# Hybrid decoder step on one core: scores, a square and the denominators' product between halves of turned probabilities, and the sampled part's order in the slots of a layer

## The chip, the core and the metric

The kernel runs on one core of a Trainium2 chip. The metric is the device time of one launch in microseconds (us), the median of several executions. The engines are named as in the profile: PE is TensorE (PEld its weight load), DVE VectorE, ACT ScalarE, POOL GpSimd, SP SyncE.

## The reference

One inference step of a hybrid decoder trunk of two layers, on a prompt of 1024 tokens and on 8 sampled sequences of 4 new tokens with 8192 tokens of paged cache each. What matters here is the mixer that each layer begins with:

```
p = h @ w_in                                   # one projection, columns split among three head groups
A: 8 heads, latent attention (latent 128, rotary key 32 shared by the heads)
   s  = (q_lat . ckv + q_rope . kr) * ATTN_SCALE, causal; pr = softmax(s); o = pr @ ckv
   for the samples the keys are 64 pages of 128 rows per sequence, read through page_table
B: 4 RWKV-7 heads of 64:  S <- S(diag(w) - kk^T (a*kk)) + v k^T,  y = S r, group norm, bonus, gate
C: short convolution of width 3
h = LN(alpha*h + concat(A,B,C) @ w_out);  h = LN(alpha*h + HierMoE(h))
```

All arithmetic is float32.

## The kernel before

Each of the two layers is a projection (in the first layer up to about 326 us), then the mixer, then the output projection and the routing, then 32 experts. The change touches the mixer alone, which the rows below show at 326 to 841 us and at 1768 to 2284 us.

The mixer of a layer is eight **slots** of code that is written out by hand, one function for each engine: the order in which `slot(w, x, y, t, b)` calls its steps is the order of the instructions on that engine, and the engines meet at counting semaphores (each step adds one to the semaphore of its engine and stage; tables such as `PE_A`, `DVE_ATT` and `ACT_SEAM` list the steps in the order in which they count, so they change with the code). Slot 0 has a function of its own (`first_slot`), slots 1 to 7 share `slot`, and each of the eight ends in `end_of_slot` and a `seam`. In slot i five strands are woven together:

- x is prompt tile i in group B. Its steps are `gramD`, `gram23`, `gram4` (products of keys), then a triangular inverse by squaring: `sq(0)`, `rr(0)`, `sq(1)`, `rr(1)`, `sq(2)`, `rr(2)`, `off1`, `off2`, `off3`. Each is 8 or 16 products of 64x64 on PE, whose result DVE (the `rr` and `off` steps) or ACT (the `sq` steps) brings back into `grams` before the next link starts. Then `mv` (values, and the bonus `cst,lw`, which ACT copies to `mv` and `bon`), `wt`, `u`, `st`.
- t is attention of prompt tile i-1, so with nk = i tiles of keys, 1 to 7. For each head h: `s(h)` scores (`kcat,qcat`) on PE, then on DVE the mask and the row's lowest (L3022, to `S_all`), `p(h)` the exponential on ACT (L2275), `pt(h, half)` the turning of the probabilities on PE (`cst,S_all`), which ACT copies to `PT` (L1974), and for each pair of heads `pv` (`PT,vrow`). `pt(h, 0)` is the first four tiles of keys, `pt(h, 1)` the rest: it is empty in the slots up to nk = 4. The turned probabilities land in two PSUM banks, `Q[0]` and `Q[1]`. At the end `R` (`cst,rden`) multiplies out the denominators and `a` on DVE applies them (`PT<-ps,PT`).
- b is sampled sequence i in group A. `both(g)` (`cst,ckvr`, two for each of four groups of pages) turns the cached latents, `scores(g)` (`krT,grams`, `grams,qcurs`), on DVE `s(g)` (L3052), `max(g)`, `ropes(g)` (L3044, `krT<-krr`), on ACT `exp(g)`, on PE `v(g)`. POOL fetches the pages (`S_all<-in_cache_ckv`) and their rotary keys (`krr<-in_cache_kr`); the fourth pages of a sequence wait for the last transposition `pt(7, ...)` on PE, and the convolution of the tile and two `krr` gathers stand behind them on POOL.
- w is the tile before in group B at its end (`hnx`, `yn`, and on PE `mixT`, `cst,mix`), y the next tile at its beginning (`sg`, `ssx`, `th`, `ssq`).

Every product stands on lines 1008 and 1011 and every copy of ACT on line 1974, in helpers; so rows are told apart by their tiles.

## Time and profile before

| | |
|---|---|
| median of 3 runs | 2915.4 us (2912.5, 2915.8, 2915.4) |
| the profiled execution | 2936.7 us, of which the span is 2934.7 us |
| mean granted clock of PE | 0.964 |
| PE busy | 2673.3 us, 91% of the span |
| DVE, ACT, POOL busy | 43%, 28%, 25% |
| the two mixers (515 and 516 us) | PE busy 477.6 and 478.4 us, granted clock 1.00 |

The span is the stretch in which the profile has instructions. A row of the timeline gives start, duration, engine, line, operation, output and input tiles, the shape and how many instructions were joined in it; in brackets stands how long the engine had been idle before it and what it waited for.

### The profile page before, as it was taken

Reading aid. Unit: us, or ns where it says so; the run is one execution under the profiler, and the core shown is the slowest. Engines: PE = TensorE matmul, PEld = TensorE weight load, DVE = VectorE, ACT = ScalarE, POOL = GpSimd, SP = SyncE. Lnnn points to the kernel's source line nnn. Section 1 sums busy time; section 2 is a strip of 40 time slices with the busy share of each in tenths; the row PEclk is TensorE's granted clock in tenths of the full one; section 3 lists DMA queues with packets and bytes.
Section 4 is the critical chain, followed back from the end, with each engine's and each line's share of the span. In section 5 each row is a group of like instructions: output and inputs, shape, how many; then the busy total and the mean of one; then the engine's idle time right before and its main releaser. Section 6 shows DMA issues by size and latency. Waiting matters only on the chain.

```text
span 2934.7 us, 55370 instructions
## 1 busy us (share of the span) xinstructions
PE 2673.3 (91%) x22106; PEld 1439.4 (49%) x22106; DVE 1247.3 (43%) x3354; ACT 833.8 (28%) x2025; POOL 744.0 (25%) x808
## 2 busy tenths in 40 slices
PE   7999889999999959999599998999999996799996
PEld 4445566666655523333244456666666454233332
DVE  4213665555543542222451255565554446222224
ACT  0111455555532001111101015555555210011113
POOL 1000322221110035555310002322211000555543
PEclk9999999999999969999799999999999997899998
DMA  8212434332242539998751133343322326599985
GB/s 300 73 35 56 157 108 119 100 100 92 74 142 90 234 139 347 374 359 313 251 212 48 38 112 123 110 116 120 97 90 76 130 77 252 208 370 355 334 307 207
DMA packets 171810, 502.19 MB, mean 171 GB/s; under 512 B 48388, under 2 KB 89608, under 8 KB 146344
## 3 DMA queue, kind: packets, MB, share of 16 engines
q1 hardware_dynamic: 105624, 321.28, 31.7%
q0 software_dynamic: 50240, 120.23, 12.0%
q10 hardware_dynamic: 15696, 57.15, 4.9%
q8 instruction: 180, 2.95, 0.4%
q14 instruction: 70, 0.57, 0.1%
HBM read 629.15 MB, written 86.89 MB: 244 GB/s over the span
## 4 chain that ended last, share of the span: by engine, by line
PE 78%; DVE 9%; ACT 3%; another core or an unknown queue 3%; DMA 3%; issue 2%; DVEq 2%; POOL 0%; POOLq 0%; ACTq 0%; SPq 0%
PE ps L1011 70%; PE ps L1008 8%; ACT PT L1974 1%; DVE grams L2543 1%; DVE S_all L3022 1%; DMA xd<-o_x 1%; DMA ybd<-yb 1%; ACT S_all L2275 1%; DMA l_b<-ybd,dga 0%; ACT grams L1974 0%; DVE PT L3052 0%; DMA c_x<-xd 0%; DVE krT L3044 0%; DVE uu L2543 0%
## 5 line engine op out<-in xcount | busy, mean ns | idle before, releaser
L1011 PE MATMUL ps<-w_slots,xbT 128*64 128x512 f32 (+1 forms) x2048 | 461.7, 604 | 19.0 <-DVE xbT L3465 19.0
L1011 PE MATMUL ps<-hT,w_in 128*128 128x512 f32 x896 | 392.0, 595 | 1.2 <-ACT hT L1974 1.2
L912 POOL DMA_INDIRECT xb<-xd,idall x256 | 256.9, 1004 | 145.0 <-issue 81.0
L1011 PEld LDWEIGHTS ps<-w_slots,xbT 128*64 128x64 f32 x2048 | 144.5, 139 | 290.9 <-issue 271.4
L1011 PEld LDWEIGHTS ps<-hT,w_in 128*128 128x128 f32 x896 | 167.8, 190 | 203.4 <-issue 200.0
L1011 PE MATMUL ps<-w_out,o_mixT 128*128 128x512 f32 (+1 forms) x640 | 243.4, 561 | 1.3 <-DVE o_h L3271 1.3
L1011 PE MATMUL ps<-w_slots,hidT 128*64 128x512 f32 (+1 forms) x1024 | 233.6, 596 | 8.5 <-issue 6.9
L3465 DVE STREAM_TRANSPOSE xbT<-xb 128x1024 f32<-128x1024 f32 x64 | 79.7, 1245 | 323.2 <-DMA xb<-xd,idall 316.2
L818 POOL TENSOR_TENSOR lnt<-lnt,cst 128x1 f32<-128x1 f32 x36 | 37.3, 1037 | 518.6 <-DVE lnt L2552 518.6
L1011 PE MATMUL ps<-grams 64*64 64x64 f32 (+1 forms) x3536 | 140.7, 225 | 27.3 <-DVE grams L2543 24.8
L1011 PE MATMUL ps<-kcat,qcat 96*128 96x512 f32 (+3 forms) x384 | 151.6, 503 | 5.9 <-DVE low L3022 5.9
L1011 PEld LDWEIGHTS ps<-w_slots,hidT 128*64 128x64 f32 x1024 | 80.4, 138 | 150.8 <-issue 143.0
L1011 PEld LDWEIGHTS ps<-w_out,o_mixT 128*128 128x128 f32 (+1 forms) x640 | 99.2, 177 | 108.7 <-issue 104.4
L1974 ACT ACTIVATE PT<-ps 128x512 f32<-128x512 f32 (+3 forms) x208 | 102.4, 492 | 173.4 <-PE ps L1008 137.1
L1008 PE MATMUL ps<-cst,S_all 128*128 128x128 f32 x832 | 136.9, 284 | 16.0 <-ACT PT L1974 13.6
L1011 PEld LDWEIGHTS ps<-grams 64*64 64x64 f32 (+1 forms) x3536 | 121.5, 138 | 51.8 <-issue 38.8
L3022 DVE CUSTOM_DVE_ANT_0 S_all<-ps,window 128x256 f32<-128x256 f32 (+7 forms) x128 | 96.7, 755 | 113.5 <-PE ps L1011 113.4
L1974 ACT ACTIVATE grams<-ps 128x512 f32<-128x512 f32 (+2 forms) x234 | 105.0, 491 | 137.8 <-PE ps L1011 94.0
L2603 DVE TENSOR_SCALAR stage<-ps,omu 128x512 f32<-128x512 f32 x32 | 23.9, 748 | 272.4 <-PE ps L1011 272.4
L1974 ACT ACTIVATE yb<-ps 128x512 f32<-128x512 f32 x64 | 38.2, 597 | 351.4 <-DMA ybd<-yb 257.4
L2275 ACT ACTIVATE S_all<-S_all,low 128x256 f32<-128x256 f32 (+7 forms) x128 | 98.9, 773 | 125.2 <-DVE low L3022 124.9
L818 POOL TENSOR_TENSOR gn<-gn,cst 128x4 f32<-128x4 f32 (+1 forms) x36 | 36.8, 1024 | 377.8 <-DVE gn L2985 332.6
(444 smaller groups left out, 4157.8 us busy)
## 6 DMA issues: line engine op xcount, KB each, us to landing
w_slots<-in_w_gu SPq DMA_DIRECT2D x64, 2048.0 KB
w_slots<-in_w_dn SPq DMA_DIRECT2D x64, 1024.0 KB
ybd<-yb ACTq DMA_DIRECT2D x64, 512.0 KB
pd<-stage SPq DMA_DIRECT2D x56, 256.0 KB, 2.5
w_in<-in_w_in SPq DMA_DIRECT2D x6, 2048.0 KB, 24.3
out_y<-c_h ACTq DMA_DIRECT2D x18, 512.0 KB, 3.3
o_mixT<-mixd SPq DMA_DIRECT2D x18, 512.0 KB, 4.0
xd<-o_x ACTq DMA_DIRECT2D x18, 512.0 KB, 2.9
```

Source lines behind the costliest of these rows:

```text
L818: return pool.tensor_tensor(x, x, mh.to_broadcast(shape), ALU.pow)
L912: pool.indirect_dma_start(xb[p % 2][:, 256 * q:256 * q + 256], None, x_quarters, bass.IndirectOffsetOnAxis(ap=idall[:, NE * q + p:NE * q + ...
L1008: return pe.transpose(out, in_, ident[s, s])
L1011: return pe.matmul(out, lhsT, rhs, start=start, stop=stop, skip_group_check=True)
L1974: return act.activation(out, in_, ACT.Copy)
L2275: self.done(act.activation(S_sb[h % 2][:, :keys], S_sb[h % 2][:, :keys], ACT.Exp, bias=low[:, h:h + 1], scale=-1.0, accum_out=den[:, h:h + ...
L2543: return dve.tensor_tensor(out, x, y, op)
L2603: dve.tensor_scalar(dst[:], src, omu[:, f:f + 1], None, ALU.mult)
L3022: dve.tensor_tensor_reduce(S_sb[h % 2][:, :keys], src, window[:, SEQ - keys:], -SCALE, HIGH, ALU.add, ALU.min, low[:, h:h + 1])\
L3465: dve.transpose(xbT[p % 2][:].rearrange("p (c i t) -> p i c t", c=8, i=4), xb[p % 2][:].rearrange("p (i c t) -> p i c t", c=8, i=4)).then_ ...
```

## The change

Steps change their place among their neighbours; one wait is added on ACT and one on DVE, and no work is added or removed.

- In the attention of slots 5 to 7, PE computes the scores `s(3)` between the halves of `pt(1)`, and `s(7)` between the halves of `pt(5)`, with `rr(0)` behind the second half. DVE, before it applies the mask to `s(3)` and `s(7)`, waits for the second half as well. ACT computes `p(2)` before it copies `pt(1, 0)`, in all slots.
- `sq(2)` stands ahead of `pt(7, 0)` on PE and ACT, and `R` between the halves of `pt(7)`. ACT's copy of `R` waits also for the last `pv`.
- On DVE `s(7)` stands ahead of `rr(0)`; `rden`, `rr(1)`, `ropes(0)`, `ropes(1)`, `rr(2)`, `a` follow in this order (before: `rr(1)`, `rden`, `a`, `ropes(0)`, `rr(2)`, `ropes(1)`).
- At the end of a slot PE has `off3` ahead of `mv`, DVE `off2` ahead of `s(0)` and `off3` ahead of `sg`, `ssx` and `max(0)`, and ACT has `th` and `ssq` behind `both(2)`.

```diff
--- before.py
+++ after.py
...
-DVE_ATT = "1s0 1s1 1s2 1s3 1s4 1s5 1s6 1s7 1rden 1a 2r0 2r1".split()
+DVE_ATT = "1s0 1s1 1s2 1s3 1s4 1s5 1s6 1s7 1rden 2r0 2r1 1a".split()
...
-PE_A = ("2gramD 2gram23 2sq0 2gram4 2rr0 1mixT 2sq1 2rr1 2sq2 2rr2 2off1 2off2 2mv 2off3 2wt "
+PE_A = ("2gramD 2gram23 2sq0 2gram4 2rr0 1mixT 2sq1 2rr1 2sq2 2rr2 2off1 2off2 2off3 2mv 2wt "
...
-ACT_SEAM = "2th 2ssq 1off2 1mv 1wt 1u0 2kk 1u1 1y 2lora 2cq 2mlaT 2gate 2qn 2exps 2kn 2V 2qrT 2tokm".split()
-DVE_SEAM = ("1off2 2sg 2ssx 1off3 2rows 1st0 1st1 2kkx 2logs 2qr 2kk2 2rkv").split()
+ACT_SEAM = "1off2 2th 2ssq 1mv 1wt 1u0 2kk 1u1 1y 2lora 2cq 2mlaT 2gate 2qn 2exps 2kn 2V 2qrT 2tokm".split()
+DVE_SEAM = ("1off2 1off3 2sg 2ssx 2rows 1st0 1st1 2kkx 2logs 2qr 2kk2 2rkv").split()
...
+                if i < NPT:
+                    first, second = (lambda h: pts[h][:1]), (lambda h: pts[h][1:])
+                    T["pe_b"].plan(("att", l, i - 1), ["s0", "s1"] + pts[0] + ["s2"] + first(1) + ["s3"] + second(1) + ["pv0"] + pts[2] + ["s4"]
+                                   + pts[3] + ["s5", "pv1"] + pts[4] + ["s6"] + first(5) + ["s7"] + second(5) + ["pv2"] + pts[6]
+                                   + first(7) + ["R"] + second(7) + ["pv3"])
...
-                    begun = ["p0", "pt0.0", "p1"] + pts[0][1:] + ["pt1.0", "p2"] + pts[1][1:] + ["p3"] + pts[2]
+                    begun = ["p0", "pt0.0", "p1"] + pts[0][1:] + ["p2"] + pts[1] + ["p3"] + pts[2]
...
@@ -1671,8 +1677,8 @@
                 x.off2()
                 b.both(2)
                 b.scores(0)
+                x.off3()
                 x.mv()
-                x.off3()
                 b.both(3)
                 x.wt()
                 b.both(4)
@@ -1701,8 +1707,8 @@
                 t.s(2)
                 x.V()
                 t.pt(1, 0)
+                t.s(3)
                 t.pt(1, 1)
-                t.s(3)
                 t.pv(0)
                 t.pt(2, 0)
                 x.qrT()
@@ -1721,20 +1727,20 @@
                 t.s(6)
                 x.gram4()
                 t.pt(5, 0)
+                t.s(7)
+                t.pt(5, 1)
                 x.rr(0)
-                t.pt(5, 1)
-                t.s(7)
                 w.mixT()
                 x.sq(1)
                 t.pv(2)
                 t.pt(6, 0)
                 x.rr(1)
                 t.pt(6, 1)
+                x.sq(2)
                 t.pt(7, 0)
-                x.sq(2)
+                t.R()
                 t.pt(7, 1)
                 t.pv(3)
-                t.R()
                 x.rr(2)
                 end_of_slot(x, y, b)
 
@@ -2284,6 +2290,7 @@
 
                 def R(self):
                     act.wait_ge(pe_b.sem, pe_b.at(self.k, "R"))
+                    act.wait_ge(pe_b.sem, pe_b.at(self.k, f"pv{NH // 2 - 1}"))
                     self.done(cp(R_sb, Q[0]), "R")
 
             class Sample:
@@ -2358,8 +2365,8 @@
                 t.p(1)
                 x.kn()
                 t.pt(0, 1)
+                t.p(2)
                 t.pt(1, 0)
-                t.p(2)
                 t.pt(1, 1)
                 x.V()
                 t.p(3)
@@ -2382,8 +2389,8 @@
                 x.sq(1)
                 t.pt(6, 0)
                 t.pt(6, 1)
+                x.sq(2)
                 t.pt(7, 0)
-                x.sq(2)
                 t.pt(7, 1)
                 t.R()
                 end_of_slot(x, y, b)
@@ -2393,11 +2400,11 @@
                 x.off1()
                 if sample:
                     sample.mixT()
-                y.th()
-                y.ssq()
                 b.both(1)
                 x.off2()
                 b.both(2)
+                y.th()
+                y.ssq()
                 x.mv()
                 b.both(3)
                 b.exp(0)
@@ -3018,6 +3025,8 @@
                     if h == 0:
                         dve.wait_ge(window_in, 16 * (self.l + 1))
                     dve.wait_ge(pe_b.sem, pe_b.at(self.k, f"s{h}"))
+                    if self.nk > 4 and self.i + 1 < NPT and h in (3, 7):
+                        dve.wait_ge(pe_b.sem, pe_b.at(self.k, f"pt{h - 2}.1"))
                     src = ps[:, 2048:2048 + keys] if self.nk > 4 else Q[h % 2][:, :keys]
                     dve.tensor_tensor_reduce(S_sb[h % 2][:, :keys], src, window[:, SEQ - keys:], -SCALE, HIGH, ALU.add, ALU.min, low[:, h:h + 1])\
                         .then_inc(dve_b.sem, dve_b.mark(self.k, f"s{h}"))
@@ -3147,12 +3156,12 @@
 
             def end_of_slot(x, y, b):
                 x.off1()
+                x.off2()
                 b.s(0)
-                x.off2()
-                b.max(0)
+                x.off3()
                 y.sg()
                 y.ssx()
-                x.off3()
+                b.max(0)
                 b.turned(0)
                 b.s(1)
                 b.max(1)
@@ -3190,15 +3199,15 @@
                 t.s(6)
                 x.gram4()
                 w.yn()
+                t.s(7)
                 x.rr(0)
-                t.s(7)
                 x.sq(1)
+                t.rden()
                 x.rr(1)
-                t.rden()
+                b.ropes(0)
+                b.ropes(1)
+                x.rr(2)
                 t.a()
-                b.ropes(0)
-                x.rr(2)
-                b.ropes(1)
                 end_of_slot(x, y, b)
 
             def choose(l, m, n, step=None):
```

On PE, the first place is the middle of slot 6 of the first layer: from `pt(5, 0)` (`cst,S_all` x4) to `mixT` (`cst,mix`). Before:

```order
L1008 MATMUL ps<-cst,S_all 128x128 x4
L1011 MATMUL ps<-grams 64x64 x8
L1008 MATMUL ps<-cst,S_all 128x128 x2
L1011 MATMUL ps<-kcat,qcat 128x512
L1011 MATMUL ps<-kcat,qcat 128x256
L1008 MATMUL ps<-cst,mix 128x128 x2
```

and now:

```order
L1014 MATMUL ps<-cst,S_all 128x128 x4
L1017 MATMUL ps<-kcat,qcat 128x512
L1017 MATMUL ps<-kcat,qcat 128x256
L1014 MATMUL ps<-cst,S_all 128x128 x2
L1017 MATMUL ps<-grams 64x64 x8
L1014 MATMUL ps<-cst,mix 128x128 x2
```

The scores `s(7)` (`kcat,qcat`) stand two pieces of work earlier, and `rr(0)` (`grams` x8) is now the last before `mixT`.

On PE, the second place is later in that slot, from `pt(6, 0)` to `rr(2)`. Before, `pt(6, 1)` and `pt(7, 0)` follow each other (`cst,S_all` x6), then come `sq(2)`, `pt(7, 1)`, `pv(3)`, `R`:

```order
L1008 MATMUL ps<-cst,S_all 128x128 x4
L1011 MATMUL ps<-grams 64x64 x8
L1008 MATMUL ps<-cst,S_all 128x128 x6
L1011 MATMUL ps<-grams 64x64 x8
L1008 MATMUL ps<-cst,S_all 128x128 x2
L1011 MATMUL ps<-PT,vrow 64x128 x12
L1011 MATMUL ps<-cst,rden 64x128 x8
L1011 MATMUL ps<-grams 64x64 x8
```

and now:

```order
L1014 MATMUL ps<-cst,S_all 128x128 x4
L1017 MATMUL ps<-grams 64x64 x8
L1014 MATMUL ps<-cst,S_all 128x128 x2
L1017 MATMUL ps<-grams 64x64 x8
L1014 MATMUL ps<-cst,S_all 128x128 x4
L1017 MATMUL ps<-cst,rden 64x128 x8
L1014 MATMUL ps<-cst,S_all 128x128 x2
L1017 MATMUL ps<-PT,vrow 64x128 x12
L1017 MATMUL ps<-grams 64x64 x8
```

`sq(2)` has moved ahead of `pt(7, 0)`, and `R` (`cst,rden`) ahead of `pt(7, 1)`. On DVE the same place, from the addition of `rr(1)` to that of `off1`, reads before (`rden`, then `a` with `PT<-ps,PT`, then the transpositions of the rotary keys around `rr(2)`):

```order
L2543 TENSOR_TENSOR grams<-grams,ps 128x256
L3027 RECIPROCAL rden<-den 128x8
L2543 TENSOR_TENSOR PT<-ps,PT 128x512
L3044 STREAM_TRANSPOSE krT<-krr 128x512
L2543 TENSOR_TENSOR grams<-grams,ps 128x256
L3044 STREAM_TRANSPOSE krT<-krr 128x512
L2875 COPY grams<-ps 128x256
```

and now:

```order
L3036 RECIPROCAL rden<-den 128x8
L2550 TENSOR_TENSOR grams<-grams,ps 128x256
L3053 STREAM_TRANSPOSE krT<-krr 128x512 x2
L2550 TENSOR_TENSOR grams<-grams,ps 128x256
L2550 TENSOR_TENSOR PT<-ps,PT 128x512
L2882 COPY grams<-ps 128x256
```

`rr(2)`, the `grams<-grams,ps` that stood between the two transpositions, now follows both, and `a` stands behind it; `rr(1)`, the first row before, now follows `rden`.

The third place is the end of the slot. On DVE, from `off1`'s copy to `off3` before:

```order
L2875 COPY grams<-ps 128x256
L3052 ISA PT,smg<-ps,window 128x512
L3052 ISA smg 128x1
L2543 TENSOR_TENSOR grams<-grams,ps 128x256
L3059 COPY smg<-smg 32x1 x3
L3061 COPY smg<-snmx 32x1
L3063 TENSOR_REDUCE smg<-smg 32x1
L3066 COPY sneg<-smg 32x1 x4
L2709 TENSOR_SCALAR sg<-sg 128x128
L2720 TENSOR_SCALAR ss<-ss 128x2
L2543 TENSOR_TENSOR grams<-grams,ps 128x256
```

and now:

```order
L2882 COPY grams<-ps 128x256
L2550 TENSOR_TENSOR grams<-grams,ps 128x256
L3061 ISA PT,smg<-ps,window 128x512
L3061 ISA smg 128x1
L2550 TENSOR_TENSOR grams<-grams,ps 128x256
L2716 TENSOR_SCALAR sg<-sg 128x128
L2727 TENSOR_SCALAR ss<-ss 128x2
L3068 COPY smg<-smg 32x1 x3
L3070 COPY smg<-snmx 32x1
L3072 TENSOR_REDUCE smg<-smg 32x1
L3075 COPY sneg<-smg 32x1 x4
```

`off2` (the first `grams<-grams,ps`) stands ahead of the mask of the sampled scores (`PT,smg<-ps,window`), `off3` (the second) directly behind it. On PE, from the sampled scores to the first of `wt`, before:

```order
L1011 MATMUL ps<-grams,qcurs 32x512 x4
L1011 MATMUL ps<-tokm,grams 64x64 x8
L1011 MATMUL ps<-cst,lw 64x2 x4
L1011 MATMUL ps<-grams 64x64 x8
L1008 MATMUL ps<-cst,ckvr 128x128 x8
L1011 MATMUL ps<-grams,tokm 64x64 x2
```

and now:

```order
L1017 MATMUL ps<-grams,qcurs 32x512 x4
L1017 MATMUL ps<-grams 64x64 x8
L1017 MATMUL ps<-tokm,grams 64x64 x8
L1017 MATMUL ps<-cst,lw 64x2 x4
L1014 MATMUL ps<-cst,ckvr 128x128 x8
L1017 MATMUL ps<-grams,tokm 64x64 x2
```

`off3` (`grams` x8) stands ahead of `mv` (`tokm,grams` and `cst,lw`) and no longer between `mv` and `both(3)`.

## Rows read from the trace of the kernel before

**Rows 1.** The head of the profile's page.

```profile
span 2934.7 us, 55370 instructions
```

**Rows 2.** Busy time in windows: stretch, its length, PE, PEld, DVE, ACT, POOL, clock.

```profile
326.00:841.00 515.00, 477.55 (x7173) 330.02 (x7173) 293.71 (x999) 289.55 (x742) 122.22 (x150) 1.00 0.34 107
1768.00:2284.00 516.00, 478.43 (x7151) 330.57 (x7147) 293.20 (x997) 289.94 (x742) 122.18 (x150) 1.00 0.34 105
```

**Rows 3.** Waits of PE, 326 to 841 us: total, times, longest.

```profile
PE ps L1011 <- DVE grams L2543: 18.6, 32, 0.9
```

**Rows 4.** Timeline of PE, end of slot 6, first layer.

```profile
720.89 0.63 PE L1008 MATMUL ps<-cst,S_all 128*128 128x128 f32 x4 [0.56 <-ACT PT L1974]
...
723.11 1.53 PE L1011 MATMUL ps<-PT,vrow 128*64 128x128 f32 x24 [0.47 <-ACT PT L1974]
724.47 1.04 PE L1011 MATMUL ps<-cst,rden 128*64 128x128 f32 x16
...
727.86 0.68 PE L1011 MATMUL ps<-cst,grams 64*64 64x64 f32 x16 [0.71 <-DVE grams L2543]
...
731.83 1.06 PE L1008 MATMUL ps<-cst,ckvr 128*128 128x128 f32 x8 [0.25 <-ACT grams L1974]
...
735.42 0.40 PE L1011 MATMUL ps<-cst,lw 128*64 128x2 f32 x8
736.42 0.68 PE L1011 MATMUL ps<-grams 64*64 64x64 f32 x16 [0.59 <-DVE grams L2543]
...
738.78 0.27 PE L1011 MATMUL ps<-grams,tokm 64*64 64x64 f32 x2 [0.66 <-DVE grams L2543]
```

**Rows 5.** Timeline of DVE, the same stretch.

```profile
726.19 0.69 DVE L2543 TENSOR_TENSOR PT<-ps,PT 128x512 f32<-128x512 f32 x1 [5.80 <-ACT PT L1974]
...
735.06 0.69 DVE L3052 CUSTOM_DVE_ANT_0 PT<-ps,window 128x512 f32<-128x512 f32 x1 [5.11 <-PE ps L1011]
...
735.85 0.42 DVE L2543 TENSOR_TENSOR grams<-grams,ps 128x256 f32<-128x256 f32 x1
...
738.31 0.42 DVE L2543 TENSOR_TENSOR grams<-grams,ps 128x256 f32<-128x256 f32 x1
```

**Rows 6.** Timelines of DVE and PE, middle of slot 6.

```profile
711.55 0.96 DVE L3022 CUSTOM_DVE_ANT_0 S_all<-ps,window 128x768 f32<-128x768 f32 x1 [1.23 <-PE ps L1011]
...
713.00 0.68 PE L1011 MATMUL ps<-grams 64*64 64x64 f32 x16 [0.51 <-DVE grams L2543]
714.12 0.44 PE L1008 MATMUL ps<-cst,S_all 128*128 128x128 f32 x2 [0.43 <-ACT PT L1974]
...
715.69 0.38 PE L1008 MATMUL ps<-cst,mix 128*128 128x128 f32 x2
...
714.26 0.43 DVE L2543 TENSOR_TENSOR mix<-uu,vrow 128x256 f32<-128x256 f32 x1
```

**Rows 7.** Timelines of ACT, POOL and PE around two `mv`, slots 6 and 1.

```profile
737.10 0.17 ACT L1974 ACTIVATE bon<-ps 128x4 f32<-128x4 f32 x1 [3.52 <-PE ps L1011]
...
722.92 1.02 POOL L870 DMA_INDIRECT S_all<-in_cache_ckv,pidx  x1 [16.56 <-PE ps L1008]
...
735.51 0.96 POOL L874 DMA_INDIRECT krr<-in_cache_kr,pidx  x1 [0.30 <-issue]
...
1837.56 0.40 PE L1011 MATMUL ps<-cst,lw 128*64 128x2 f32 x8
...
1838.01 0.17 ACT L1974 ACTIVATE bon<-ps 128x4 f32<-128x4 f32 x1 [2.29 <-PE ps L1011]
...
1838.35 1.00 POOL L874 DMA_INDIRECT krr<-in_cache_kr,pidx  x1 [0.34 <-issue]
```

**Rows 8.** Timelines of ACT and PE, beginning of slot 4.

```profile
553.15 0.59 ACT L1974 ACTIVATE PT<-ps 128x512 f32<-128x512 f32 x1
553.63 0.71 ACT L2275 ACTIVATE S_all<-S_all,low 128x512 f32<-128x512 f32 x1
...
553.89 1.09 PE L1011 MATMUL ps<-PT,vrow 128*64 128x128 f32 x16
```

More of the change, by code:

```diff
@@ L187 @@
 DVE_SATT = "s0 m0 T0 s1 m1 r2 o0 T1 s2 m2 r3 o1 T2 s3 m3 o2 T3 o3".split()
-DVE_ATT = "1s0 1s1 1s2 1s3 1s4 1s5 1s6 1s7 1rden 1a 2r0 2r1".split()
+DVE_ATT = "1s0 1s1 1s2 1s3 1s4 1s5 1s6 1s7 1rden 2r0 2r1 1a".split()
 DVE_SATT0 = "r0 r1".split()
-PE_A = ("2gramD 2gram23 2sq0 2gram4 2rr0 1mixT 2sq1 2rr1 2sq2 2rr2 2off1 2off2 2mv 2off3 2wt "
+PE_A = ("2gramD 2gram23 2sq0 2gram4 2rr0 1mixT 2sq1 2rr1 2sq2 2rr2 2off1 2off2 2off3 2mv 2wt "
         "2u0 2st0 2u1 2st1").split()
 PE_S = ("q kkb qlat qrT tokm gramD gram23 new sq0 gram4 rr0 sq1 rr1 sq2 rr2 off1 off2 mv off3 wt").split()
-PE_S0 = ("2mlaT 2lora 1u0 2kks 2q 2kkb 2kn 2V 1y2 2qrT 1st0 2tokm 2gramD 2gram23 2sq0 2gram4 2rr0 2sq1 2rr1 2sq2 2rr2 2off1 1mixT 2off2 2mv 2off3 2wt "
+PE_S0 = ("2mlaT 2lora 1u0 2kks 2q 2kkb 2kn 2V 1y2 2qrT 1st0 2tokm 2gramD 2gram23 2sq0 2gram4 2rr0 2sq1 2rr1 2sq2 2rr2 2off1 1mixT 2off2 2off3 2mv 2wt "
          "2u0 2st0 2u1 2st1").split()
@@ L281, in plan @@
                     T["pe_b"].plan(("satt", l, i - 1), PE_SATT[-1:])
-                T["pe_b"].plan(("att", l, i - 1), ["s0", "s1"][i == NPT:] + sum([pts[h] + ([f"s{h + 2}"] if h + 2 < NH else []) + ([f"pv{h // 2}"] if h % 2 else [])
+                if i < NPT:
[3 more added lines that the diff above has]
+                                   + first(7) + ["R"] + second(7) + ["pv3"])
+                else:
+                    T["pe_b"].plan(("att", l, i - 1), ["s1"] + sum([pts[h] + ([f"s{h + 2}"] if h + 2 < NH else []) + ([f"pv{h // 2}"] if h % 2 else [])
                                                                       for h in heads], []) + ["R"])
                 if i < NPT:
-                    begun = ["p0", "pt0.0", "p1"] + pts[0][1:] + ["pt1.0", "p2"] + pts[1][1:] + ["p3"] + pts[2]
+                    begun = ["p0", "pt0.0", "p1"] + pts[0][1:] + ["p2"] + pts[1] + ["p3"] + pts[2]
                 else:
```

## The prediction

> **What bounds the kernel now.** The page's head gives the span, 2934.7 us [rows 1]; the profiled execution took 2936.7 us, 0.7% above the median of the runs, 2915.4 us, so the sum is made on the span and then taken from the median. Windows come next, since the change touches the two mixers alone: of 1031 us PE is busy 956.0 us, so it is idle for 75 us, and its clock is 1.00 [rows 2]. DVE, ACT and POOL are busy for 57%, 56% and 24% of these windows. PE sets the pace, no busy time is removed, and the most that any reordering could give is those 75 us. What PE waits for is seen in its waits: in the first mixer 18.6 us in 32 waits are for DVE's `grams` [rows 3]. The timeline then shows where, and with whom PE waits. Slot 6 stands for the others [rows 4 to 6].
>
> **The change, by its places on PE.**
>
> Before `off1` PE waits 0.71 us [rows 4], in all 14 of the slots 1 to 7. It waits for DVE's addition of `rr(2)`, and DVE is late because `a` runs from 726.19 to 726.88 and a transposition of `krr` behind it, before `rr(2)`'s turn comes [rows 5]. `rr(2)`'s product ends under `both(0)`; with `a` behind it and both transpositions ahead, DVE is free when that product ends. What `a` brings (the mixed output) nobody on PE waits for before the next slot. 14 x 0.71 = 9.9 us.
>
> Before `off3` PE waits 0.59 us [rows 4], in all 16 ends of slots. `off2`'s addition on DVE starts at 735.85, because the mask of the sampled scores starts at 735.06 ahead of it [rows 5], though `off2`'s product had ended before `both(2)` began at 731.83 [rows 4]. Now it comes ahead of the mask. 16 x 0.59 = 9.4 us.
>
> Before `wt` PE waits 0.66 us [rows 4] (0.33 to 0.91 in the 16 places, mostly 0.66). `off3`'s addition starts at 738.31 on DVE [rows 5], behind `max(0)` and `sg`. Now `off3`'s product stands 0.4 + 0.6 us earlier against `both(3)` and its addition directly behind the mask. 16 x 0.66 = 10.6 us, if nothing takes the place of this wait; what may, stands in a part of its own below.
>
> Before `both(2)` (731.83) PE waits 0.25 us for an ACT copy [rows 4], in 12 places. ACT's `th` and `ssq` stood ahead of `both(1)`'s copy and now stand behind `both(2)`'s. 12 x 0.25 = 3.0 us.
>
> In slots 5 to 7, `pt(7, 0)` waits 0.56 us (0.46 to 0.67) for the copy that frees its bank, and `pv(3)` 0.47 us for the last copy [rows 4]. `sq(2)`, 0.6 us of products that wait for nothing in this stretch, now fills the first. The second wait stays about as it is: `R` (1.04 us) [rows 4] now covers `pt(7, 0)`'s copy but stands before the half whose copy `pv(3)` needs. 6 x 0.56 = 3.4 us.
>
> In the same slots, PE waits 0.51 us before `rr(0)` and 0.43 us before `pt(5, 1)`, and the scores stand behind [rows 6]. Now `s(7)` can start when DVE has read `s(6)`, at 711.55 + 0.96 = 712.51, and a signal of some 0.1 later. With 1.3 us for the scores (they start 0.28 after `pt(5, 1)`'s 714.12 and end at 715.69), 0.3 for `pt(5, 1)` and 0.6 for `rr(0)`, `mixT` is due at 714.8. It needs DVE's last step of `yn`, which ends at 714.69 [rows 6] plus a signal, so it starts at 714.8 to 715.0 in place of 715.69. I take 0.7 us; 6 x 0.7 = 4.2 us. The bounds are nothing (yn later, since DVE's `s(7)` moved) and 0.94, both waits. In slots up to 4 there is no second half and this gives nothing.
>
> A price is on ACT: the copy of `pt(1, 0)` now stands behind `p(2)`. In slot 4 the copy starts at 553.15, `p(2)` at 553.63 with 0.71 us, and PE's `pv(0)` at 553.89, right behind the copy [rows 8]. There `pv(0)` moves by the 0.7; in slot 3 about 0.3; slots 1 and 2 have slack; in slots 5 to 7 the scores `s(3)` that moved in between cover it, and a wait at the second half moves to `pv(0)`. Two layers: 2 x (0.7 + 0.3) = 2.0 us. Bounds: 0, and 14 x 0.7 = 9.8 if it shows in every slot.
>
> So far: 9.9 + 9.4 + 10.6 + 3.0 + 3.4 + 4.2 - 2.0 = 38.5 us.
>
> **What takes the place of the wait before `wt`.** `wt` needs `off3` from DVE and `mv` from ACT. Before, `mv` had 0.6 us of `off3` and the wait of 0.59 more behind it, now only `both(3)`. By the rows, `mv`'s last product (`cst,lw`) ends at 735.42 + 0.40 = 735.82, yet ACT, idle for 3.52 us, starts its copy at 737.10 [rows 4, 7]: 1.28 us late. In 14 of 16 places it is 0.5 to 2.1 us late. In slot 1 of the second layer it is not: the product ends at 1837.96 and the copy starts at 1838.01 [rows 7]. What differs is POOL. In slot 6 the second `krr` gather runs until 736.47 [rows 7], and ACT moves 0.63 later; in slot 1 POOL's first `krr` gather starts only at 1838.35, after the product. In the 14 late places the copy starts 0.6 us after the second gather's end (once earlier). So I read that PE's signal is held from about 0.7 us after the first gather's start until 0.6 after the second's end, some 2.2 us.
>
> After the signal ACT needs 0.07 + 0.38 and about 0.15 to hand on, 0.6 us; `both(3)` gives 1.0 us of cover. A signal late by L thus opens a gap of L - 0.4. With today's median of 1.3 in all 16 it would be 14 us. But the gathers move too. They follow the page gather at 722.92, which is released by the last transposition `pt(7, ...)` [rows 7], by the convolution's steps, whose time is the same within a us or so in all slots. Between that transposition and `mv` the change takes out 0.6 (`sq(2)`, slots up to 4) or 1.0 (`R`, slots 5 to 7), 0.71 and 0.25 of waits, and puts 0.6 (`off3`) in: `mv` comes 1.0 to 1.35 us earlier against the gathers. Shifting the 14 slots by that, the product ends before the hold in ten; it falls into it in four, and in the two first slots, whose gathers are not tied to `pt(7)`. Six places at about 1.9 - 0.4 = 1.5 us: 9.0 us. Bounds: 0, and 16 x 1.7 = 27 (2.1, the largest lateness seen, less 0.4).
>
> The end of a PE row is itself in question. The Trainium skill, Perfetto Trace Analysis (Tensor Engine Instruction), says that the profiler's end of a matmul is an estimate and not an observation. By the drawn ends alone there would be no lateness and the sum were 38.5; by ACT's start it is 29.5. I go by ACT, since the difference comes and goes with POOL's gathers.
>
> **Sum.** 38.5 - 9.0 = 29.5 us: span 2934.7 to 2905.2, median 2915.4 to 2886.
>
> **Rivals.**
>
> 1. The late signal is covered or vanishes: 38.5 us, 2877. For it: slot 1 of the second layer, and that most places move out of the hold. Against it: 14 of 16 late today. 0.15.
>
> 2. The waits around the turned halves stay. `Q[0]` and `Q[1]` are all the banks there are, and a half waits for the copy of one before whatever stands between; work put between delays that half's copy, and `pv` waits longer. For it: `pv(3)`'s 0.47, which no edit removes [rows 4]. Then the terms of `pt(7, 0)` and of `s(7)`, 3.4 + 4.2, fall away: 29.5 - 7.6 = 21.9, 2893.5. 0.15. The Trainium skill, Perfetto Trace Analysis (Optimization Strategy), says that a gap which repeats on the busiest engine can mean too few buffers for the next tile. The repeated 0.56 fits that sentence, and by it reordering would not help there.
>
> 3. The signal is held in all 16 places, as it nearly is today, because the gathers follow PE's pace rather than `pt(7)`. 16 x 1.5 = 24, gain 14.5, 2901. 0.12.
>
> 4. Slower: the same mechanism, harder. If the hold begins with `mv` in every end of a slot and lasts its whole 2.2 us and the wait for POOL's next instruction besides, the gap passes 38.5 / 16 = 2.4 us, that is L above 2.8 us; above 3.2 the kernel is 0.2% slower: with L = 3.5 the change costs 16 x 3.1 - 38.5 = 11 us, 2926. Against it: no row has L over 2.1. 0.07.
>
> 5. No change that can be told: the waits leave these places and reappear at the next step that PE shares with DVE, since the chain of `rr` and `off` steps, not PE's other work, sets the slot's length. Against it: PE is idle for only 75 of 1031 us, so its work sets the length, and each late link has other products of about 1 us beside it [rows 2, 4]. 2915. 0.08.
>
> **Chances and range.** Forecast 0.43, rivals 0.15, 0.15, 0.12, 0.07, 0.08. A difference within 0.2% (5.8 us) can't be told from none in this kernel. Faster is the forecast with rivals 1 to 3, 0.85; same 0.08; slower 0.07. The range reaches from beyond rival 1 to beyond rival 3: 2873 to 2906, with 0.85 in it before the sizes' own error.
>
> **What would show it.** In the profile of the changed kernel the waits of 0.71 before `off1` and 0.59 before `off3` are gone in all slots. `off3`'s addition on DVE stands directly behind the mask. `pt(7, 0)` has no wait, `pv(3)` one of about 0.5, `mixT` starts 0.7 earlier. Before `wt` there is no wait in about ten places and one for ACT's `mv` of 1 to 2 us in about six; `bon` starts right behind `cst,lw` in the ten. `pv(0)` in slots 3 and 4 has a new wait for ACT. PE's idle time in the two windows falls from 75 to about 45 us. The prediction is wrong if waits for `mv` stand in most slots, or if the removed waits come back at `scores(1)`, `u(0)` or `v(0)`.

## The result and the profile after

The changed kernel takes 2872.1 us (median of 5 runs, 2871.2 to 2879.8) against 2915.8 us before (5 runs, 2912.5 to 2925.4). The ratio is 0.985, 95% interval 0.983 to 0.987: by the ratio 44.9 us faster, 39 to 51. The forecast was 2886, with 2873 to 2906 as range; the time lies 0.9 us below the range, and the gain was half as large again as the forecast one, 29.5 us. One execution of `e_noswap` below (2940.5 us, mean granted clock 0.921, against 0.966 to 0.969 in its other five) is left out of its median.

The head of the changed kernel's page, and its windows over the two mixers (stretch, length, busy time of PE, PEld, DVE, ACT, POOL, clock):

```profile
span 2870.5 us, 55398 instructions
...
326.00:820.00 494.00, 475.43 (x7181) 329.89 (x7177) 294.76 (x1000) 290.17 (x742) 122.28 (x150) 1.00 0.36 111
1742.00:2234.00 492.00, 473.65 (x7175) 328.54 (x7174) 294.33 (x1000) 290.36 (x742) 122.19 (x150) 1.00 0.36 112
```

PE is now idle for 986.0 - 949.1 = 36.9 us in the two mixers, before for 75.0 [rows 2]. Its busy time fell too, from 956.0 to 949.1 us for the same products. The waits of PE in the first of them (total, times, longest):

```profile
PE ps L1017 <- ACT PT L1980: 7.2, 10, 1.3
PE ps L1014 <- DVE mix L2550: 3.2, 4, 1.1
PE ps L1017 <- DVE low L3031: 2.0, 4, 0.7
PE ps L1014 <- ACT PT L1980: 1.6, 3, 0.9
...
PE ps L1017 <- DVE grams L2550: 0.6, 2, 0.5
```

The group that stood first, 18.6 us in 32 waits for DVE's `grams` [rows 3], is 0.6 us in 2. What leads now is the wait for ACT's copies to `PT`, ahead of the `pv` products.

PE's timeline of the end of slot 6 in the first layer, to be held against [rows 4] (a line `...` stands for rows left out):

```profile
705.89 0.63 PE L1014 MATMUL ps<-cst,S_all 128*128 128x128 f32 x4
706.45 1.09 PE L1017 MATMUL ps<-cst,rden 128*64 128x128 f32 x16
707.47 0.44 PE L1014 MATMUL ps<-cst,S_all 128*128 128x128 f32 x2
708.38 1.53 PE L1017 MATMUL ps<-PT,vrow 128*64 128x128 f32 x24 [0.47 <-ACT PT L1980]
...
710.46 1.09 PE L1014 MATMUL ps<-cst,ckvr 128*128 128x128 f32 x8
711.48 0.68 PE L1017 MATMUL ps<-cst,grams 64*64 64x64 f32 x16
...
717.14 1.06 PE L1017 MATMUL ps<-grams,qcurs 128*32 128x512 f32 x8
718.14 0.68 PE L1017 MATMUL ps<-grams 64*64 64x64 f32 x16
718.65 0.63 PE L1017 MATMUL ps<-tokm,grams 64*64 64x64 f32 x16
719.22 0.40 PE L1017 MATMUL ps<-cst,lw 128*64 128x2 f32 x8
719.55 1.09 PE L1014 MATMUL ps<-cst,ckvr 128*128 128x128 f32 x8
720.57 0.27 PE L1017 MATMUL ps<-grams,tokm 64*64 64x64 f32 x2
```

The waits of 0.56 (`pt(7, 0)`), 0.71 (`off1`), 0.59 (`off3`) and 0.66 (`wt`) are gone, in all slots. `pv(3)` keeps its 0.47. DVE and ACT in the same stretch:

```profile
718.38 0.69 DVE L3061 CUSTOM_DVE_ANT_0 PT<-ps,window 128x512 f32<-128x512 f32 x1 [2.72 <-PE ps L1017]
719.00 0.08 DVE L3061 DVE_READ_ACCUMULATOR2_ANT smg<- 128x1 f32 x1
719.18 0.42 DVE L2550 TENSOR_TENSOR grams<-grams,ps 128x256 f32<-128x256 f32 x1
...
719.66 0.17 ACT L1980 ACTIVATE bon<-ps 128x4 f32<-128x4 f32 x1 [1.73 <-PE ps L1017]
719.73 0.38 ACT L1980 ACTIVATE mv<-ps 128x256 f32<-128x256 f32 x1
```

`off3`'s addition ends at 719.60, `mv`'s copy at 720.11, and `wt` starts at 720.57 without waiting for either. ACT starts `bon` 0.04 us after the end of `cst,lw` (719.62), in all 16 places: the late signal to which the prediction gave 9.0 us is not there.

Two more readings of these rows. From `both(0)` to `off1` PE now needs 711.48 - 710.46 = 1.02 us; before it needed 727.86 - 726.06 = 1.80 (`both(0)` began at 726.06 in the timeline of before). That is 0.78 us less, though the wait was 0.71: products of one piece overlap the last of the piece before by 0.07 us, and a wait costs this overlap too. And from the sampled scores to `wt` it is 720.57 - 717.14 = 3.43 us, before 738.78 - 733.82 = 4.96: 1.53 less for waits of 1.25. (The scores began at 733.82 in the timeline of before.)

One loss in the changed kernel's profile is not a wait. In slot 1 of the first layer the granted clock falls to its lower level (0.51 of full speed, 1.2 GHz, from 378 to 380 us, and 0.64 on the mean from 380 to 382), where before it stays at 1.00. In the 14 us up to 378 PE was busy for 10.2 us, with waits of up to 1.31 us; before, it was busy for 10.4 of the 14 us up to 380, with waits of up to 0.92, and the clock did not fall. The windows of PE at this place (columns as above) and the products of `sq(1)`, before first, then changed:

```profile
366.00:390.00 24.00, 19.70 (x389) 15.61 (x389) 15.99 (x51) 13.13 (x43) 3.41 (x5) 1.00 0.34 99
379.83 1.15 PE L1011 MATMUL ps<-grams 64*64 64x64 f32 x32
```

```profile
366.00:390.00 24.00, 21.15 (x400) 17.32 (x400) 14.67 (x45) 11.93 (x35) 3.71 (x5) 0.93 0.31 93
378.02 1.98 PE L1017 MATMUL ps<-grams 64*64 64x64 f32 x32
```

The same products take 1.98 in place of 1.15 us, and the slot lasts 58.0 us where the same slot of the second layer, at full clock, lasts 56.6. This 1.4 us comes back in some of the experiments.

### The profile page after: what moved, and what is told of

Its sections match the earlier page's. It is cut to its first block, busy times and chain, and to the rows that moved or that the text cites. A ratio compares the mean times of both kernels' runs of the same rounds, so it can differ in the third digit from the quotient of the medians.

```text
span 2870.5 us, 55398 instructions
## 1 busy us (share of the span) xinstructions
PE 2654.7 (92%) x22106; PEld 1438.3 (50%) x22106; DVE 1247.9 (43%) x3354; ACT 834.9 (29%) x2025; POOL 743.5 (26%) x808
## 4 chain that ended last, share of the span: by engine, by line
PE 82%; DVE 8%; DMA 3%; ACT 2%; issue 2%; DVEq 2%; POOL 0%; POOLq 0%; ACTq 0%; SPq 0%
PE ps L1017 73%; PE ps L1014 9%; DVE S_all L3031 1%; DMA xd<-o_x 1%; ACT PT L1980 1%; DMA c_x<-xd 1%; DMA w_slots<-in_w_gu,rowA 1%; ACT S_all L2281 1%; DMA l_b<-ybd,dga 0%; DMA ybd<-yb 0%; DVE uu L2550 0%; DVE r_e L2550 0%; DVE l L2764 0%; DVE grams L2550 0%; DVE c_x L2592 0%
## 5 line engine op out<-in xcount | busy, mean ns | idle before, releaser
L1017 PE MATMUL ps<-w_slots,hidT 128*64 128x512 f32 (+1 forms) x1024 | 232.6, 593 | 10.4 <-issue 8.5
```

The costliest lines, as they stand in the source:

```text
L1017: return pe.matmul(out, lhsT, rhs, start=start, stop=stop, skip_group_check=True)
```

## The experiments

The kernel before was run along with each group of experiments: 2917.7 us with `again`, `e_end`, `e_rotary` and `e_att`, 2915.7 with `e_noswap`, `e_p2`, `e_fill` and `e_fill2`, 2917.0 with `e_sq`, `e_s7`, `e_best` and `e_best2`. Each ratio stands with its 95% interval. Where slots are compared, the length of one is that from the end of one `mv` (`cst,lw`) to the next, worked out from the rows of each profile, and before is the profile of `again`.

### 1. The kernel before, once more (`again`)

No edit.

> The kernel of before once more, unchanged. Theory 1 (the late start of ACT's bon copy after mv belongs to the one execution that was profiled, which at 2936.7 us was also 0.7% above the median): the new profile shows bon right behind cst,lw (0.05 us) in most of the 16 places, a span near 2915 us, and the waits of PE before off1, off3 and wt (0.71, 0.59, 0.66) unchanged. Theory 2 (the kernel before has the late signal in every execution, and the new order removes it): 12 or more of the 16 places are late again by 0.5 to 2.1 us.

Measured: 2920.9 us, ratio 1.001 (0.999 to 1.003). The profile of this execution, ACT, POOL and PE around `mv` in slot 6 (to be held against [rows 7]):

```profile
735.63 0.17 ACT L1974 ACTIVATE bon<-ps 128x4 f32<-128x4 f32 x1 [2.29 <-PE ps L1011]
...
734.93 0.96 POOL L874 DMA_INDIRECT krr<-in_cache_kr,pidx  x1 [0.30 <-issue]
...
735.18 0.40 PE L1011 MATMUL ps<-cst,lw 128*64 128x2 f32 x8
736.17 0.68 PE L1011 MATMUL ps<-grams 64*64 64x64 f32 x16 [0.59 <-ACT mv L1974]
736.78 1.09 PE L1008 MATMUL ps<-cst,ckvr 128*128 128x128 f32 x8
738.54 0.28 PE L1011 MATMUL ps<-grams,tokm 64*64 64x64 f32 x2 [0.66 <-DVE grams L2543]
```

`cst,lw` ends at 735.58, in the middle of the second `krr` gather (734.93 to 735.89), and ACT starts at 735.63. In 11 of the 16 places the product ends within a `krr` gather. ACT starts 0.04 to 0.05 us after it in all 16 places here, and in all 16 of each of the other twelve profiles of this study, the changed kernel's among them. The late signal stood in one execution, that of the rows. Theory 1 holds. (That execution, 2936.7 us, was also slower than the median, but not by the signals: up to the last `mv` the two profiles are 0.6 us apart, at 2260.8 and 2260.2 us, and nearly all the 14 us by which the spans differ lie behind it.) The waits of 0.59 and 0.66 are the same in both executions; the first is put down to `ACT mv` here only because `mv` is now the last event before it, while what PE waited for was `off2`'s addition.

### 2. The three parts alone (`e_end`, `e_rotary`, `e_att`)

`e_end` takes from the diff of the change only the hunks of `end_of_slot` (only its steps of PE, then of DVE, are shown):

```diff
                 b.scores(0)
+                x.off3()
                 x.mv()
-                x.off3()
...
                 x.off1()
+                x.off2()
                 b.s(0)
-                x.off2()
-                b.max(0)
+                x.off3()
                 y.sg()
                 y.ssx()
-                x.off3()
+                b.max(0)
```

with ACT's `th` and `ssq` behind `both(2)`. `e_rotary` takes the order on DVE of `rden`, `rr(1)`, `ropes`, `rr(2)`, `a`. `e_att` takes the rest: `s(3)`, `s(7)`, `sq(2)`, `R`, `p(2)`, with the new waits of DVE and ACT.

> Only the end of a slot is changed (off3 ahead of mv on PE, off2, s(0), off3, sg, ssx, max(0) on DVE, th and ssq behind both(2) on ACT); all else is before. Theory 1 (each removed wait gives back its length plus the 0.07 us by which one product overlaps the next when PE doesn't stop): 16 x (0.59 + 0.66) + 12 x 0.25 + 44 x 0.07 = 26 us faster, no wait before wt. Rival (removed waits are worth their length only): 23 us. Theory of the prediction (mv's signal held in six or more places): 14 us or less, with waits for ACT before wt.

> Only the order on DVE of rden, rr(1), ropes(0), ropes(1), rr(2), a is changed; all else is before. Theory 1: 14 x (0.71 + 0.07) = 11 us faster. Rival (lengths only): 9.9 us. If the wait only moves on to the next link (off2 or off3): under 3 us.

> Only the attention strand is changed (s(3), s(7), sq(2) and R between the halves, p(2) ahead of the copy of pt(1, 0), s(7) ahead of rr(0) on DVE); the end of the slot and the order of the rotary keys are as before. By the prediction's terms 3.4 + 4.2 - 2.0 = 5.6 us faster; with the overlap of 0.07 for each wait removed 6 to 7 us. Rival (the waits around the turned halves only move): -2.0 to 0, so no change or slower by 2 us, all of it in slots 3 and 4 before pv(0).

| | median | ratio (interval) | gain by the ratio | both mixers, `mv` of slot 0 to `mv` of slot 7 |
|---|---|---|---|---|
| `again` | 2920.9 | 1.001 (0.999 to 1.003) | none | 481.4 + 481.8 |
| `e_end` | 2887.0 | 0.989 (0.988 to 0.991) | 30.9 | 470.1 + 469.0 |
| `e_rotary` | 2907.0 | 0.996 (0.995 to 0.998) | 11.4 | 475.9 + 476.5 |
| `e_att` | 2911.1 | 0.998 (0.997 to 0.999) | 6.4 | 478.6 + 478.3 |
| changed | 2872.1 | 0.985 (0.983 to 0.987) | 44.9 | 461.7 + 459.9 |

Read by the mixers, which vary less than the whole, the parts give 24.1, 10.8 and 6.3 us, together 41.2; the changed kernel gives 41.6. So the parts add up, and no part eats another's gain. The stretch counts seven of the eight ends of a slot. The one left out is worth 1.2 us a layer: from the last scores to `wt` it takes 3.43 us in place of 4.63, since the wait before `wt` was only 0.33 there. With it the changed kernel gains 44.0 us in the mixers and `e_end` 26.5. Both lose the 1.4 us of clock in slot 1 of the first layer, `e_rotary` and `e_att` don't.

`e_rotary` is 11 us as expected with the overlap: every slot from 1 to 7 is 0.72 to 0.83 us shorter. `e_end` was expected at 26 us, and at 23.0 without any overlap. Its 26.5 us hold the 1.4 us of clock as a loss and, as a gain, 2.2 us of the swap of experiment 4, of which neither theory knew; without both it is 25.7, which fits the first. Its time, 26 to 36 us by the interval, can't tell the two apart. No wait stands before `wt` in its profile, so the prediction's 14 or less is out.

### 3. The attention strand's terms (`e_sq`, `e_s7`)

`e_sq` is before with the second place of the change (`sq(2)` moves on ACT too), `e_s7` with the first (on DVE `s(7)` then stands ahead of `rr(0)`, with its new wait):

```diff
+                x.sq(2)
                 t.pt(7, 0)
-                x.sq(2)
+                t.R()
                 t.pt(7, 1)
                 t.pv(3)
-                t.R()
```

```diff
                 t.pt(5, 0)
-                x.rr(0)
+                t.s(7)
                 t.pt(5, 1)
-                t.s(7)
+                x.rr(0)
                 w.mixT()
```

> Before, with sq(2) ahead of pt(7, 0) on PE and ACT and R between the halves of pt(7) (ACT's copy of R waits for pv(3)); nothing else. The prediction's term is 6 x 0.56 = 3.4 us; with the overlap of 0.07 it is 3.8: slots 5 to 7 shorter by 0.6 us each, slots 1 to 4 unchanged. Rival 2 of the prediction (the copies around the turned halves set the pace, a moved square only moves the wait): nothing in slots 5 to 7.

> Before, with s(7) between the halves of pt(5) and rr(0) behind, on DVE s(7) ahead of rr(0) with its new wait; nothing else. The prediction's term is 6 x 0.7 = 4.2 us; the rows of the changed kernel show 0.57 in slot 6 (pt(5, 0) to mixT 3.28 us, before 3.85), so 3.4 us: slots 5 to 7 shorter by 0.6 each, slots 1 to 4 unchanged. Rival (yn or the new wait on DVE takes it back): nothing.

Measured: `e_sq` 2910.9 us, ratio 0.998 (0.996 to 0.999); `e_s7` 2910.4 us, 0.998 (0.996 to 0.999). Slots 5, 6, 7 of the first layer last 73.1, 77.0, 81.0 us before; with `e_sq` 72.6, 76.5, 80.4, with `e_s7` 72.8, 76.5, 80.4. Over both layers `e_sq` shortens the slots 5 to 7 by 2.9 us and `e_s7` by 3.2; slots 1 to 4 become shorter by 1.7 us with `e_sq`, half of it in slot 4, where no change was expected, and by 0.3 with `e_s7`. In slots 5 to 7 both theories hold within 0.9 us: rival 2 of the prediction falls there, since filling one wait around the turned halves didn't move it to the next. In slots 1 to 4, where there is no second half and `e_s7` only swaps `s(7)` and `rr(0)`, a wait did move: in slot 2 the 0.27 us before `rr(0)` is gone, and the wait before `mixT` is 0.96 us in place of 0.43, with nothing gained. The mixers are 4.6 and 3.5 us shorter; the whole times are 2.7 and 2.6 us better than that, but their intervals reach down to 3.5 and 1.8 us.

These two runs and `e_att` also price what is left of the attention strand. In slots 1 to 4 `e_att` is 0.9 us longer than before, where `e_sq` and `e_s7` together are 2.0 shorter: `p(2)` costs about 3.0 us. In slots 5 to 7 `e_att` is 7.3 us shorter, 1.2 more than the 6.1 of the two: that is left for `s(3)`, which has no run of its own. The rows agree: the wait of 0.69 us before `pt(1, 1)` became one of 0.46, 0.56 and 0.67 us before `pv(0)` in slots 5, 6 and 7.

A word on that rival: the description ahead of the prediction says that the turned probabilities land in `Q[0]` and `Q[1]`. The code (`pt`) turns all of them into `Q[2]`; `Q[0]` and `Q[1]` hold the scores. So the case for waits was stronger than the prediction made it, one bank and not two, and the rival fell all the same: a copy of 0.6 us and its signals fit under one piece of other work.

### 4. Is the swap of `mv` and `off3` on PE needed? (`e_noswap`)

```diff
                 b.scores(0)
-                x.off3()
                 x.mv()
+                x.off3()
                 b.both(3)
```

> The changed kernel with PE's mv ahead of off3 again; DVE and ACT keep the new order. Theory 1 (the waits before off3 and wt came from DVE's order alone; off3's addition needs about 0.7 us and both(3) behind it lasts 1.0): no wait comes back, and the time is that of the changed kernel but for about 0.1 us a slot (in the changed kernel mv's products start 0.51 us after off3's, where 0.61 was usual), so 0 to 3 us slower than the changed kernel. Rival (the swap on PE carries the gain before wt): 16 x 0.66 = 10 us slower than the changed kernel.

Measured: 2872.5 us, ratio 0.985 (0.982 to 0.988), the same as the changed kernel. PE and DVE at the end of slot 6:

```profile
718.10 1.06 PE L1017 MATMUL ps<-grams,qcurs 128*32 128x512 f32 x8
719.10 0.68 PE L1017 MATMUL ps<-tokm,grams 64*64 64x64 f32 x16
719.71 0.40 PE L1017 MATMUL ps<-cst,lw 128*64 128x2 f32 x8
720.04 0.68 PE L1017 MATMUL ps<-grams 64*64 64x64 f32 x16
720.65 1.09 PE L1014 MATMUL ps<-cst,ckvr 128*128 128x128 f32 x8
721.67 0.27 PE L1017 MATMUL ps<-grams,tokm 64*64 64x64 f32 x2
...
720.77 0.42 DVE L2550 TENSOR_TENSOR grams<-grams,ps 128x256 f32<-128x256 f32 x1 [0.72 <-PE ps L1017]
```

No wait comes back. `off3`'s addition starts 0.05 us after its product's end (720.72) and is done at 721.19, before `both(3)` is. So the 0.59 and the 0.66 did not come from PE's order. ACT's new order is in this kernel too, but it is DVE's additions that both waits stood behind [rows 4, 5]. The swap is worth 721.67 - 718.10 = 3.57 against 3.43 us, 0.14 a slot or an estimated 2.2 us in 16 (1.6 in the mixers, where slot 4 of the first layer goes the other way), because `off3` directly ahead of `mv` holds PE for 0.51 us and `mv` behind it for 0.57, where each takes 0.61 apart.

### 5. ACT's copy of `pt(1, 0)` (`e_p2`)

```diff
-                t.p(2)
                 t.pt(1, 0)
+                t.p(2)
                 t.pt(1, 1)
```

> The changed kernel with ACT's copy of pt(1, 0) ahead of p(2) again, as before; all else is changed. Theory (the prediction's term of -2.0, seen as 0.2 and 0.4 us longer slots 4 and 3): 1 to 2 us faster than the changed kernel, with the slots 1, 2 and 5 to 7 as they are. Rival (the waits of 0.5 to 1.3 us before pv(0) in all 14 slots come from this edit): 5 us or more faster.

Measured: 2865.0 us, ratio 0.983 (0.981 to 0.985). Slots 2, 3, 4 become 0.1, 0.6 and 0.4 to 1.0 us shorter, slots 5 to 7 stay within 0.14: 3.0 us in both layers, slot 1 of the first layer apart. That slot lasts 56.6 us in `e_p2`, at a clock of 1.00, so its 1.4 us are the clock's. The rest of the 7 us by which the median is lower isn't in the mixers' slots, and its interval overlaps that of the changed kernel. PE in slot 4, of the changed kernel first and of `e_p2` below:

```profile
544.85 1.02 PE L1017 MATMUL ps<-kcat,qcat 96*128 96x512 f32 x2
546.49 1.09 PE L1017 MATMUL ps<-PT,vrow 128*64 128x128 f32 x16 [0.61 <-ACT PT L1980]
```

```profile
544.35 1.02 PE L1017 MATMUL ps<-kcat,qcat 96*128 96x512 f32 x2
545.30 1.09 PE L1017 MATMUL ps<-PT,vrow 128*64 128x128 f32 x16
```

The prediction's mechanism was right: `pv(0)` waits 0.61 us behind the later copy. Its size was 2.0, measured 3.0, the same as by the difference in experiment 3. In slots 5 to 7 the earlier `p(2)` gives nothing.

### 6. Filling the rest (`e_fill`, `e_fill2`, `e_best`, `e_best2`)

```diff
                 t.pt(1, 1)
+                x.qrT()
                 t.pv(0)
                 t.pt(2, 0)
-                x.qrT()
...
                 t.pt(7, 1)
+                x.rr(2)
                 t.pv(3)
-                x.rr(2)
```

`e_fill` has both pieces. `e_fill2` has `sq(1)` ahead of `mixT` as well, and the copy of experiment 5 in the slots up to 4. `e_best` is `e_p2` with the second piece alone; `e_best2` is `e_best` with `sq(1)` ahead of `mixT`.

> The changed kernel, and on PE qrT also ahead of pv(0) (from between pt(2, 0) and pt(2, 1)) and rr(2) ahead of pv(3). Theory (a wait for ACT is filled by any product that is ready): the waits before pv(0), 0.5 to 1.3 us in 14 slots, and before pv(3), 0.4 to 0.5 us in 6, are gone; with a wait of 0.5 that comes back before pt(2, 1) in 6 slots, 8 to 12 us faster than the changed kernel. Rival (ACT, not the order on PE, sets this part of the slot): the wait moves to pt(2, 0) or s(4), and the gain is under 3 us.

> As e_fill, with sq(1) ahead of mixT on PE and, where nk is up to 4, ACT's copy of pt(1, 0) ahead of p(2). mixT waits 1.1, 0.7, about 0.6 and 0.5 us for DVE's yn in slots 1 to 4, which sq(1) (1.1 us) can fill: 5 to 6 us less than e_fill, and 1 us for the copy. Rival (rr(1) then waits for the square by as much): no faster than e_fill.

> The changed kernel with ACT's copy of pt(1, 0) ahead of p(2) and rr(2) ahead of pv(3) on PE. Against the kernel with the copy alone (2865 us, mixers 458.5 and 458.7 us): the wait of 0.37 to 0.47 before pv(3) in slots 5 to 7 is filled, 6 x (0.44 + 0.07) = 3 us, so 2862 us and mixers of 457. Rival (rr(2) needs DVE's rr(1) and the copy of sq(2), which are then late): the wait stands before rr(2), no gain.

> As e_best, with sq(1) ahead of mixT on PE. Theory: the waits of 1.1, 0.7, 0.6 and 0.5 us before mixT in slots 1 to 4 are filled by sq(1) (1.1 us), 5 us less than e_best. Rival: sq(1) needs DVE's addition of rr(0), or ACT takes mixT before the square's copy, and the wait moves to sq(1) or rr(1): within 1 us of e_best.

| | median | ratio (interval) | both mixers |
|---|---|---|---|
| `e_fill` | 2885.7 | 0.989 (0.987 to 0.992) | 470.8 + 467.3 |
| `e_fill2` | 2880.2 | 0.987 (0.985 to 0.990) | 464.6 + 462.1 |
| `e_best` | 2860.1 | 0.981 (0.978 to 0.983) | 458.9 + 457.4 |
| `e_best2` | 2855.7 | 0.980 (0.978 to 0.983) | 454.1 + 453.9 |

`e_fill` missed: both theories forecast a gain, and it is 13.6 us slower than the changed kernel (16.5 in the mixers). Slot 4, PE and ACT:

```profile
551.58 1.02 PE L1017 MATMUL ps<-kcat,qcat 96*128 96x512 f32 x2
553.69 1.08 PE L1017 MATMUL ps<-cst,qr 64*32 64x64 f32 x32 [1.09 <-ACT vrow L1980]
...
552.49 0.58 ACT L1980 ACTIVATE PT<-ps 128x512 f32<-128x512 f32 x1
552.96 0.58 ACT L1980 ACTIVATE vrow<-ps 128x512 f32<-128x512 f32 x1
```

`qrT` needs the bank that ACT frees with its `vrow` copy, which stands behind the very copy that `pv(0)` waits for. The piece put into the gap was later than what it was to cover, a wait of 1.09 us in place of 0.61. Part of the 16.5 us is clock. In slot 1 PE waits 1.78 us before `qrT`, and the granted clock falls to 0.50 right behind it, in both layers: the mean clock of this slot is 0.89 and 0.94. These two slots alone are 3.9 and 2.4 us longer than in the changed kernel, the other twelve 0.6 to 1.1 us each.

`e_fill2`'s median is 5.5 us below that of `e_fill`, 6 to 7 having been expected, but their intervals overlap. Its slots 2 to 4 are 0.6 to 0.8 us shorter, and another 6.0 us are in the two slots 1, where less clock is lost.

`sq(1)` and `rr(2)` are of the other kind, their inputs long there. With `rr(2)` moved, PE in slot 6 of `e_best` goes through without a stop:

```profile
705.10 1.09 PE L1017 MATMUL ps<-cst,rden 128*64 128x128 f32 x16
706.12 0.44 PE L1014 MATMUL ps<-cst,S_all 128*128 128x128 f32 x2
706.49 0.68 PE L1017 MATMUL ps<-grams 64*64 64x64 f32 x16
707.10 1.53 PE L1017 MATMUL ps<-PT,vrow 128*64 128x128 f32 x24
708.56 1.09 PE L1014 MATMUL ps<-cst,ckvr 128*128 128x128 f32 x8
```

Slots 5 to 7 are 0.4 to 0.6 us shorter each than in `e_p2`, 3.2 us in all, as expected. But in slots 1 to 4, where `pv(3)` had no wait to fill, six of the eight are 0.11 to 0.15 us longer, and slot 1 of the first layer loses 1.4 us of clock again, so the mixers as a whole are only 0.9 us shorter than in `e_p2`. In `e_best2` the waits before `mixT` (0.51 in slot 4 of the changed kernel) are gone too: slots 1 to 4 lose 2.0, 0.7, 0.8, 0.7 us in the first layer and 0.5, 0.7, 0.8, 0.9 in the second. With slots 5 to 7 it is 8.2 us in the mixers, of which 1.4 are clock that `e_best` lost and `e_best2` didn't; 6.8 are left, where 5 was expected. Its median, 2855.7 us, is the lowest of the study. Against the changed kernel it is 16 us lower, though the two ratios' intervals just touch at 0.983, and 13.5 us shorter in the mixers, of which 1.4 are clock. Against `e_best` alone the intervals don't part them, the slots do.

## Why the prediction was right or wrong

**What bounds the kernel, and the most to be had.** Right in the main: the idle time of PE fell by 38 us, from 75.0 to 36.9. But the 75 us weren't all that reordering could give. Busy time for the same products fell besides, by 6.9 us, for the most part because pieces that follow each other without a stop overlap (an estimated 4.5 us, 0.07 at each of 64 removed waits) and by the swap (2.2).

**`off1`, `off3`, `wt`, `both(2)`.** Places, causes and counts were right, and all these waits are gone. The sizes were low. A wait was priced at the bracket of its row, and its removal gives 0.07 us more, since the next piece can then overlap the end of the last. For `off1` that is 10.9 in place of 9.9 us (`e_rotary`: 10.8). For the end of the slot 23.0 us became 26.5: the overlap of 44 waits is 3.1 us and the swap 2.2, less 1.4 of clock and small differences. (The wait before `wt` was 0.33 to 1.01 us in the 16 places, not 0.33 to 0.91, 10.8 us in sum for the 10.6 of the text.)

**The price of the late signal, -9.0 us.** This is the step that failed. It was read from one execution and took something of that execution for a trait of the kernel. Its readings were right: in that execution 13 of 14 late copies start 0.61 to 0.71 us after the end of the second gather. But `again` shows `bon` 0.04 to 0.05 us after `cst,lw` in 16 of 16 places, 11 of them within a `krr` gather, and so do the other twelve profiles. What held the signals in that execution isn't known; the argument from POOL's gathers is refuted as a rule of this kernel, and not replaced. What a late signal would cost in the changed order isn't known either, since none came up in it. Rival 1, the full 38.5 us and 2877 us with a chance of 0.15, had the right case: the signal isn't late.

**`pt(7, 0)` and `s(7)`.** 3.4 was measured as 2.9 in the slots 5 to 7, with 1.7 more in slots 1 to 4 where the term had nothing, and 4.2 as 3.2: with `s(7)` ahead, `pt(5, 0)` to `mixT` takes 3.28 us where it was 3.85, 0.57 a slot and not 0.7. That `pv(3)` keeps its wait was right. Moving `s(3)` was put at nothing in slots 5 to 7 (the wait would only move to `pv(0)`); it moved and became shorter, and about 1.2 us are left for it.

**`p(2)`.** The mechanism was right. 2.0 was measured as 3.0, by `e_p2` and again by `e_att` against `e_sq` and `e_s7`. All terms of the strand together give 6.3 in the mixers, 5.6 in the prediction: errors of 0.7 to 1.2 us either way nearly cancel, which is luck.

**Rival 2.** `Q[0]` and `Q[1]` are not where the turned halves land (experiment 3), and the wait of 0.56 us that it would have kept is gone.

**The clock.** The prediction took it as 1.00 and had no term for it. The 1.4 us of slot 1 in the first layer are a loss that nothing in it covers.

**Sum.** By the three parts measured alone it is 26.5 + 10.8 + 6.3 = 43.6 us in the mixers, against 44.0 for the changed kernel and 44.9, 39 to 51, in the time. Of the 15 us between forecast and measurement 9.0 are the late signal; the other 5 to 6 are low sizes, 3.5 of them at the end of the slot, 0.9 at `off1` and 0.7 in attention. Taking the late signal away would have given 2877 us, within the range. The range missed by 0.9 us because its low end was set beyond rival 1 by 4 us only, with every wait taken at its bracket.

## What to carry to other kernels

Price a removed wait as the start of the next piece minus the start of the one before, against what this pair takes where nothing waits; the bracket alone is short by the overlap, here 0.07 us on waits of 0.25 to 0.7. Before an oddity of a single trace (a late signal, a slow copy) gets a term of its own, run the unchanged kernel again and profile it. A gap is filled only by work whose own inputs and bank are free earlier than what the gap waits for: `sq(1)`, `sq(2)` and `rr(2)` shortened the slots where a wait stood, while `qrT`, whose bank was freed by the same engine one copy later, made the wait longer. And when slots are compared between two profiles, look at the granted clock of each first: one slot of the same work differed by 1.4 us through it.
